# One block of x in SBUF, h and the experts' sums in DRAM, three slots for query-weight tiles

## What is computed

```python
h = h + mix @ w_out[i]
hn = _rmsnorm(h, ln_ffn_g[i])
h = h + _peer(hn, peer_wq[i], peer_keys[i], peer_u[i], peer_v[i])
gate = jax.nn.sigmoid(_rmsnorm(h, ple_norm_g[i]) @ ple_w_gate[i])
h = h + gate * (p[i] @ ple_w_proj[i])

# in _peer, for 8 heads of 16 experts each
q = (xt @ wq).reshape(t, PEER_HEADS, 2, PEER_HALF)
...
act = _gelu(jnp.einsum('td,thkd->thk', xb, u_tab[eb])) * gb
return jnp.einsum('thk,thkd->td', act, v_tab[eb])
```

## Time and profile before

| | us |
|---|---|
| median of 3 runs | 3350.19 |
| lowest, highest | 3345.12, 3357.08 |
| profiled execution | 3361.44 |
| its span | 3359.6 |
| busy: PE, DVE, ACT, POOL | 2811.2, 1714.6, 1663.9, 1140.8 |

### The profile page before, as it was taken

One profiled execution on the slowest core, in us unless ns is written; L12 is line 12 of the kernel. 1 busy time (PEld: TensorE's weight loads), 2 busy tenths in 40 slices (PEclk: granted clock), 3 DMA queues, 4 the chain that ended last, 5 costly groups with the idle time before them and its releaser, 6 DMA issues.

```text
span 3359.6 us, 44577 instructions
## 1 busy us (share of the span) xinstructions
PE 2811.2 (84%) x17472; PEld 2355.9 (70%) x17472; DVE 1714.6 (51%) x3924; ACT 1663.9 (50%) x3325; POOL 1140.8 (34%) x886
## 2 busy tenths in 40 slices
PE   6677877777678767577789999998999999999999
PEld 4465666565656566455478887888999997778887
DVE  6596969596877778455343555564101124621010
ACT  2167676778677767588644222233323222533231
POOL 0023332333333333233133222224645542156463
PEclk7887798878978888588889889999999999999999
DMA  5298999999999999999412000002233321023332
GB/s 188 76 398 357 369 405 408 385 374 406 404 380 379 416 416 408 415 407 393 168 53 74 14 1 1 1 1 63 82 95 88 90 75 50 1 78 98 93 95 76
DMA packets 287523, 695.75 MB, mean 207 GB/s; under 512 B 27664, under 2 KB 207299, under 8 KB 221651
## 3 DMA queue, kind: packets, MB, share of 16 engines
q0 software_dynamic: 73728, 536.90, 39.6%
q1 hardware_dynamic: 213587, 156.02, 14.7%
HBM read 689.72 MB, written 3.15 MB: 206 GB/s over the span
## 4 chain that ended last, share of the span: by engine, by line
PE 54%; DVE 23%; DMA 10%; ACT 10%; issue 3%; POOL 0%; SPq 0%; DVEq 0%; ACTq 0%; POOLq 0%
PE PS L1823 29%; DMA ring<-in_peer_uv,eidx 10%; DVE ring L1523 6%; PE PS L929 5%; ACT ring L1138 3%; PE PS L985 1%; PE PS L1725 1%; PE PS L1722 1%; DVE acc L2661 1%; PE PS L798 1%; PE PS L1715 1%; PE PS L766 1%; ACT L1131 1%; PE PS L1844 1%; PE PS L2041 1%
## 5 line engine op out<-in xcount | busy, mean ns | idle before, releaser
L929 PE MATMUL PS<-C,ring 128*128 128x128 f32 x4096 | 693.5, 320 | 355.5 <-ACT ring L1138 349.5
L929 PEld LDWEIGHTS PS<-C,ring 128*128 128x128 f32 x4096 | 552.8, 164 | 514.9 <-ACT ring L1138 459.6
L721 POOL DMA_INDIRECT ring<-in_peer_uv,eidx x512 | 487.5, 952 | 1140.2 <-PE PS L929 960.8
L1523 DVE CUSTOM_DVE_ANT_0 ring<-ring,PS 128x1024 f32<-128x1024 f32 x512 | 619.9, 1216 | 306.5 <-DMA ring<-in_peer_uv,eidx 300.2
L1138 ACT ACTIVATE ring<-ring,act_d 128x512 f32<-128x512 f32 x1024 | 683.5, 714 | 16.7
L1823 PE MATMUL PS<-held_uH,GW 128*128 128x264 f32 (+1 forms) x3008 | 661.1, 315 | 17.7 <-POOL BIG_value L2379 11.0
L2365 POOL TENSOR_TENSOR GW<-held_wr,GW 128x1024 fp32r<-128x1024 f32 x178 | 429.2, 2412 | 423.4 <-ACT GW L2130 423.4
L1823 PEld LDWEIGHTS PS<-held_uH,GW 128*128 128x128 f32 x3008 | 503.2, 193 | 57.8 <-issue 19.7
L1823 PE MATMUL PS<-BIG_value,GW 128*128 128x264 f32 (+1 forms) x1504 | 447.7, 313 | 0.0
L1823 PE MATMUL PS<-hid,GW 128*128 128x264 f32 (+1 forms) x2304 | 366.5, 321 | 0.0
L1823 PEld LDWEIGHTS PS<-hid,GW 128*128 128x128 f32 x2304 | 332.3, 188 | 33.7
(11 more groups left out here) (490 smaller groups left out, 3779.9 us busy)
## 6 DMA issues: line engine op xcount, KB each, us to landing
held_wr<-in_w_ff SPq DMA_DIRECT2D x128, 512.0 KB, 4.1
wqr<-in_peer_wq SPq DMA_DIRECT2D x32, 512.0 KB
W<-in_peer_wq SPq DMA_DIRECT2D x31, 512.0 KB
held_wr<-in_w_in_ab SPq DMA_DIRECT2D x18, 512.0 KB, 3.7
ring<-in_peer_uv,eidx POOLq DMA_INDIRECT x512
BIG<-in_w_in SPq DMA_DIRECT2D x4, 1536.0 KB, 11.5
held_wr<-in_w_qkv_c SPq DMA_DIRECT2D x12, 512.0 KB, 3.8
w_out<-in_w_out SPq DMA_DIRECT2D x1, 4096.0 KB, 19.5
```

What stands on the lines that cost most here:

```text
L721: e.indirect_dma_start(out=ring[:, i % RING, :], out_offset=None, in_=pairs, in_offset=bass.IndirectOffsetOnAxis(ap=eidx[:, blk % 2, k:k + ...
L929: ins = e.matmul(bank[6 + j // 4][:, j % 4 * P:(j % 4 + 1) * P], row[:, j * P:(j + 1) * P], ident, start=(k == 0 and j % 4 == 0), stop=(k ...
L1523: e.tensor_tensor_reduce(row, row, hn, 1.0, 0.0, ALU.mult, ALU.add, act[:, k:k + 1]).then_inc(*n.up(e_dot))
```

## The change

X keeps one block. The h of every block goes to DRAM (kept) behind the fourth query tile of the block. The sums of blocks 0 to 2 are copied by ACT into X instead of W4, and stored from there to DRAM (kept_sums) behind the fourteenth tile of the next block; then the next x is loaded into X (for block 3 its own h is loaded back). Block 1's x is loaded behind the eighth tile. PE's transposes of the sums and DVE's addition to h move from the block ends into a new part "home" of three steps ahead of each tail; both operands are loaded from DRAM with the other weights of the tail. The 4 KB of each partition that X no longer takes are a third slot, wq3, for query tiles: slots go round by three, tile 2 is requested once the first block's z is done (f_z), and counts on a semaphore that w_in had used.

The diff, cut to its core. Waits of d_p for 80 become waits for 144, tokens(blk) becomes X, and lines that only register the new parts are left out.

```diff
-NQ = 2
+NQ = 3
...
-TAIL_STEPS = 25
+TAIL_STEPS, HOME_STEPS = 25, 3
...
-            if k == 2 and blk:
-                order.append(("done", blk - 1))
...
-                others += [(("tail", b), TAIL_STEPS) for b in range(3)]
+                others += [part for b in range(3) for part in ((("home", b), HOME_STEPS), (("tail", b), TAIL_STEPS))]
...
-    late = 3 * TAIL_STEPS
+    late = 3 * (HOME_STEPS + TAIL_STEPS)
...
+    wq3 = sbuf(st, "wq3", [P, D])
...
-    X = sbuf(st, "X", [P, 2, D])
+    X = sbuf(st, "X", [P, D])
...
     def sums(blk):
-        return W4[:, 1, :] if blk < NB - 1 else W4[:, 0, :]
-
-    def sum_banks(blk):
-        return (bank[0], bank[1]) if blk < NB - 1 else (bank[6], bank[7])
-
-    def tokens(blk):
-        return X[:, blk % 2, :]
+        return X[:, :] if blk < NB - 1 else W4[:, 0, :]
 
     def fetched(blk):
-        return BIG[:, 4224 + D * blk:4224 + D * blk + D] if blk < 2 else X[:, blk % 2, :]
+        if blk == NB - 1:
+            return X[:, :]
+        return BIG[:, 4224 + D * blk:4224 + D * blk + D] if blk < 2 else wqr[:, :]
+
+    def fetched_sums(blk):
+        return BIG[:, 6272 + D * blk:6272 + D * blk + D] if blk < 2 else sinT[:, 8:16, :].rearrange("p j t -> p (j t)")
 
     def query_slot(i):
-        return rows[:, 8, :] if i == 1 else W4[:, 3, :] if i % 2 else wqr[:, :]
+        return rows[:, 8, :] if i == 1 else (wqr[:, :], W4[:, 3, :], wq3[:, :])[i % NQ]
+
+    def query_there(i):
+        return (d_wi[0], 16 * (i // NQ + 2)) if i % NQ == 2 else (d_q[i % NQ], 16 * (i // NQ + 1))
...
-    kept = nc.dram_tensor("kept", (2, P, D), F32).ap()
+    kept = nc.dram_tensor("kept", (NB, P, D), F32).ap()
+    kept_sums = nc.dram_tensor("kept_sums", (NB - 1, P, D), F32).ap()
...
             if i >= NQ:
                 e.wait_ge(r_q, i - NQ + 1)
-            if blk and m == 1:
+            if blk and m < 3 and i % NQ == 1:
                 e.wait_ge(r_hTp, 2 * blk + 2)
-            e.dma_start(query_slot(i), wqv[m]).then_inc(d_q[i % NQ], 16)
+            if i == 2:
+                e.wait_ge(f_z, 1)
+            e.dma_start(query_slot(i), wqv[m]).then_inc(query_there(i)[0], 16)
 
     def first_sync(e):
         first_loads(e)
         for i in range(16 * NB):
             query_weight(e, i)
-            if i == NQ:
-                e.dma_start(tokens(1), xv[1]).then_inc(d_x, 16)
-            b = i // 16 - 1
-            if i in (27, 43):
-                e.wait_ge(e_x, b + 1)
-                e.dma_start(kept[b], tokens(b)).then_inc(d_kept, 16)
-            if i in (29, 45):
-                e.wait_ge(d_kept, 16 * (b + 1))
-                e.dma_start(tokens(b + 2), xv[b + 2]).then_inc(d_x, 16)
+            b, m = i // 16, i % 16
+            if m == 3:
+                e.wait_ge(r_hs, b + 1)
+                e.dma_start(kept[b], X[:, :]).then_inc(d_kept, 16)
+            if b == 0 and m == 7:
+                e.wait_ge(d_kept, 16)
+                e.dma_start(X[:, :], xv[1]).then_inc(d_x, 16)
+            if b and m == 13:
+                e.wait_ge(e_sum, b)
+                e.dma_start(kept_sums[b - 1], X[:, :]).then_inc(d_kept, 16)
+                e.wait_ge(d_kept, 16 * (2 * b + 1))
+                e.dma_start(X[:, :], xv[b + 1] if b < NB - 1 else kept[b]).then_inc(d_x, 16)
...
-        for b in range(2):
+        for b in range(NB - 1):
+            e.dma_start(fetched_sums(b), kept_sums[b]).then_inc(d_p, 16)
             e.dma_start(fetched(b), kept[b]).then_inc(d_p, 16)
...
-        if blk >= 2:
-            e.wait_ge(e_x, blk - 1)
...
+    def home_tensor(e, n, blk):
+        s = Steps()
+        e.wait_ge(d_p, 144)
+        e.wait_ge(r_gate, ALL_BATCHES)
+        if blk:
+            e.wait_ge(t_hT, 2 * blk)
+        for half in range(2):
+            ins = turn(e, turn_banks(blk)[half], fetched_sums(blk), at=4 * half)
+        ins.then_inc(*n.up(e_sum))
+        yield from s.to(HOME_STEPS)
...
             elif name[0] == "end":
-                turn_sums(e, n, name[1])
+                if name[1] == NB - 1:
+                    turn_sums(e, n)
...
     def keep_sums(e, n, blk):
 
         if blk < NB - 1:
-            e.wait_ge(r_idx, NH * (blk + 1) + AHEAD)
+            e.wait_ge(d_kept, 32 * (blk + 1))
...
-            if blk and h == AHEAD:
-                e.wait_ge(e_sum, 2 * blk)
...
-    def experts_done(e, n, blk):
-        e.wait_ge(e_sum, 2 * blk + 2)
+    def add_sums(e, n, blk, banks):
+
         for c in range(2):
-            Xc = tokens(blk)[:, 512 * c:512 * c + 512]
-            ins = e.tensor_tensor(Xc, Xc, sum_banks(blk)[c], ALU.add)
+            Xc = fetched(blk)[:, 512 * c:512 * c + 512]
+            ins = e.tensor_tensor(Xc, Xc, banks[c], ALU.add)
         ins.then_inc(*n.up(e_x))
+
+    def home_vector(e, n, blk):
+        s = Steps()
+        yield from s.to(HOME_STEPS - 1)
+        e.wait_ge(d_p, 144)
+        e.wait_ge(e_sum, NB + blk)
+        add_sums(e, n, blk, turn_banks(blk))
+        yield from s.to(HOME_STEPS)
+
+    def experts_done(e, n):
+        e.wait_ge(e_sum, 2 * NB)
+        e.wait_ge(d_x, 16 * NB)
+        add_sums(e, n, NB - 1, (bank[6], bank[7]))
```

More of the change, by code:

```diff
@@ L429, in emit @@
     d_x0, d_x, d_kept = sem("d_x0"), sem("d_x"), sem("d_kept")
-    kept = nc.dram_tensor("kept", (2, P, D), F32).ap()
+    kept = nc.dram_tensor("kept", (NB, P, D), F32).ap()
+    kept_sums = nc.dram_tensor("kept_sums", (NB - 1, P, D), F32).ap()
     d_v, d_br, d_m, d_w = sem("d_v1"), sem("d_br"), sem("d_m"), sem("d_w")
     d_wi = [sem(f"d_wi{k}") for k in range(4)]
-    d_q = [sem(f"d_q{i}") for i in range(NQ)]
+    d_q = [sem(f"d_q{i}") for i in range(NQ - 1)]
     d_r = [sem(f"d_r{i}") for i in range(RING)]
@@ L651, in first_loads @@
     def first_loads(e):
-        e.dma_start(tokens(0), xv[0]).then_inc(d_x0, 16)
+        e.dma_start(X[:, :], xv[0]).then_inc(d_x0, 16)
         e.dma_start(C1[:, :], cst1).then_inc(d_v, 16)
@@ L924, in expert_sum @@
         if k == 0 and blk:
-            e.wait_ge(e_sum, 2 * blk - 1)
+            e.wait_ge(e_sum, blk)
         for j in range(8):
@@ L931, in expert_sum, with turn_sums @@
         ins.then_inc(*n.up(e_pv))
-    def turn_sums(e, n, blk):
-        e.wait_ge(e_sum, 2 * blk + 1)
-        turn(e, sum_banks(blk)[0], sums(blk))
-        turn(e, sum_banks(blk)[1], sums(blk), at=4).then_inc(*n.up(e_sum))
+    def turn_sums(e, n):
+        e.wait_ge(e_sum, 2 * NB - 1)
+        turn(e, bank[6], sums(NB - 1))
+        turn(e, bank[7], sums(NB - 1), at=4).then_inc(*n.up(e_sum))
+    def home_tensor(e, n, blk):
[8 more added lines that the diff above has]
+        yield from s.to(HOME_STEPS)
     def meta_tensor(e, n):
         e.wait_ge(r_gate, ALL_BATCHES)
-        e.wait_ge(d_p, 80)
+        e.wait_ge(d_p, 144)
         for k in range(8):
@@ L964, in tail_tensor @@
         own = project_tensor(e, n, blk)
-        e.wait_ge(e_x, max(blk + 1, NB - 1))
-        e.wait_ge(d_p, 80)
+        e.wait_ge(e_x, blk + 1)
+        e.wait_ge(d_p, 144)
         for half in range(2):
@@ L1071, in front_scalar @@
     def front_scalar(e, n, blk):
-        Xb = tokens(blk)
+        Xb = X[:, :]
         s = Steps()
@@ L1568, in first_vector @@
             parts["side", b] = side_vector(e, n, b)
+            parts["home", b] = home_vector(e, n, b)
             parts["tail", b] = tail_vector(e, n, b)
@@ L1577, in first_vector @@
             elif name[0] == "done":
-                experts_done(e, n, name[1])
+                experts_done(e, n)
             elif name in parts:
```

3 lines of the change are left out of this document (2 added, 1 removed).

## The result

The changed kernel takes 3372.62 us (median of 6 runs, 3370.29 to 3382.1), the kernel before 3350.38 us beside it (6 runs). The ratio is 1.0059, with a 95% interval of 1.0040 to 1.0079: about 20 us slower, beyond the 0.3% that a measurement can tell from no change. The forecast was 3360.8 us, +0.32%, slower: the sign is right, the size is short by 5 to 9 us by the two ratios. The first median lies 1.6 us above the range's upper end of 3371.

The account below looks back on a forecast made before the run. DMA, full during the gathers, was taken as the limit. Terms -0.4 + 0.4 + 11.6 - 2.0 + 1.0 = +10.6 us took the profiled 3361.44 to 3372.0 us, a predicted median of 3360.8 us (+0.32%), range 3351 to 3371.

Parts of the forecast that it names:

- The limit: Stage of 512 gathers, 165 to 1630 us: DMA engines busy 0.98 where 1.02 is full, so DMA bounds it.
- The third slot: PE's waits for query weights, 17.9 us in six places, mostly go; worth only -0.4 us, as gathers in flight cover them.
- block 1's first tile: Its tile request waits for the turned normed rows, so PE stops some 7 us instead of 3.9; +0.4 us (0 to 3).
- The nine net transfers: Parking x, h and sums adds net nine 512 KB transfers, 4.72 MB, to the full stage; +11.6 us (0 to 14.9).
- The block ends: Ends of blocks 0 to 2 lose transposes, DVE's wait and additions, so DMA dips there shrink; -2.0 us (0 to -3).
- The home work: End of block 3 gains the transposes and additions, 84 steps instead of 75 over 72 pairs; +1.0 us (0 to 4).
- Behind the last gather: After the last pair nothing changes, since block 3's tail reads its rows in X as before; no time added.
- The cited rate: About 358 GB/s as a core's effective rate would make the nine transfers 13.2 us; the trace's 413 GB/s disagreed.
- Partly hidden transfers: Rival: stores cost DMA less than loads, or extra bytes fall into the stage's dips; 3354.6 us, chance 0.20.
- PE's waits pay: Rival: gathers follow PE rather than bytes, so its saved waits count; about -8.3 us, 3341.9 us, chance 0.08.
- Late reads: Rival: the tail's reads arrive late, PE stops at the meta tokens, the ring isn't refilled; 3371 us, chance 0.15.

Follow-up runs that it names:

- the empty steps: Kernel before with three empty steps ahead of each of block 3's three tails, 84 steps in 72 pairs, no byte moved; ratio 1.0019 to the kernel before.
- second comparison: Changed kernel, unchanged, in twelve more runs against 35 of the kernel before; ratio 1.0046 (1.0026 to 1.0066).
- the steps apart: Changed kernel with DVE's reciprocal one step later behind ACT's root and PE's step one later behind DVE's; ratio 1.0045 to the kernel before.

## Why the prediction was right, and where it was short

**The limit.** Right. DMA stayed at 0.98 over the stage, 24 added transfers slowed the gathers by 1.0 to 1.1 us each, and 6.6 us of PE's waits could come and go (two slots or three) with no effect that the times or the gathers show.

**The third slot (-0.4 us, and +0.4 for block 1's first tile).** Right: 1.0046 with it, 1.0043 without. The wait at block 1's first tile was forecast at some 7 us and was 6.80. The advice to issue early, weighed there, gave here what the shares had said: nothing.

**The nine net transfers (+11.6 us).** Right in kind, perhaps a little high. At the 1.05 and 1.22 us measured for each, nine are 9.5 to 11 us. Six of them fall behind gather 384, five where the third slot moves a query tile ahead of it: 6.3 us for five at 413 GB/s, 7.8 us for six at 1.3 us. Block 3 to its last gather takes 378.3, 378.1 and 379.4 us in the changed kernel (its two traces and that with two slots) and 370.9 with the empty steps, a difference of 7.7 us at equal pace, and 7.5 us to the last sum. The three in blocks 0 to 2, with the block ends against them, were to be about 2 us; the scatter of 15 us hides that.

**The block ends (-2.0 us).** The shares rose as forecast, from a lack of 3.0 us against 1.02 to one of (0.02 x 14) + (0.01 x 14) + (0.01 x 16) = 0.6 us, 2.4 us less. It is read from shares only, in stretches that aren't quite the same; no run took this alone. The store and the load behind it stood 11.6 us apart and not 5, which was covered there.

**The home work (+1.0 us, bounds 0 and 4).** This is the step that was mis-sized. The term asked how much room DMA had in the last 190 us and priced the added PE and DVE instructions by it. What cost most was not the added work but the quicker pace: 84 steps in 72 pairs put steps of the tail into one pair that had been in two. Empty steps alone, with no instruction in them, cost 6 us (1 to 12) by the ratio, 2 to 3 us by the gathers' issue times and 3.8 us to the last sum. In the changed kernel the term is about 5 us, the part of block 3's 11.2 us that its bytes don't explain, above the forecast's bound of 4. The rows of the change show the moved steps at pair 56; nothing in the forecast asked which waits such a move makes. With 5 in place of 1.0 and 9.5 to 11.6 for the transfers the forecast's sum is 12.5 to 14.6 us (an estimate), which is within the second comparison's 9 to 22 us, and at the lower end of the first one's 13 to 26.

**Behind the last gather (nothing).** This is open in part. Nothing there was changed, and the forecast put nothing. The changed kernel and its variants took 1720.9 to 1742.1 us there (table), the kernel before and its variants 1721.8 to 1732.4. The difference comes and goes with the granted PE clock in the next 600 us. Rows of 350 us from 250 us behind the last gather, of the changed kernel's second trace and of the one with the steps apart:

```profile
1891.00:2241.00 350.00, 321.27 (x2430) 281.02 (x2429) 203.66 (x577) 100.33 (x283) 81.21 (x80) 0.89 0.00 1
```

```profile
1889.00:2239.00 350.00, 319.31 (x2556) 278.56 (x2555) 215.82 (x607) 104.48 (x295) 85.23 (x84) 0.94 0.00 1
```

At 0.89 PE does 2430 matmuls in the time in which it does 2556 at 0.94, and the whole behind the last gather is 1742.1 against 1720.9 us. The same spread, at 0.90 and 0.94, is in the kernel before and in that with the empty steps. Whether the changed kernel falls more often on the low side isn't settled by one trace of each, but every run's mean granted clock is on record. Over the fast runs it is 0.888 and 0.889 in the changed kernel (6 and 11 runs) and 0.893 in the kernel before beside the second (35 runs); it is 0.890 with the empty steps, 0.891 with the two slots. Among those 35 runs one with 0.001 less is about 1.5 us longer (an estimate from a straight line through them), so 0.004 less would go with some 6 us, of the 15 and 20 measured. A part of that is block 3 itself, where the clock is 0.85 against 0.88 in the stretch from 1440 to 1630. What else holds the clock lower in the changed kernel, and whether it is cause or company of the longer time, no run shows.

**The cited rate.** The 358 GB/s that the forecast took from the Trainium skill, "HBM Reference", section "Specifications (TRN2)", stands there as a core's share when both cores of a pair stream. For a core alone the same section has about 425 GB/s, and the 413 GB/s of the earlier trace rows lie near that: the page and this trace, of one core, don't disagree.

**The rivals.** Partly hidden transfers (3354.6 us): the price per transfer leans that way by 6 to 24%, within its error, stores aren't free as it needed, and the time is far above it. PE's waits pay (3341.9): refuted by the sign of the result and by the added transfers; the two-slot kernel agrees. Late reads (3371): refuted, as the reads were there 24 us early; the median near that number came about in another way.
